# Other home addresses in SBUF for the operands of a split-fp32 transformer step

## The reference

```python
x += 1/2 * g1 * SwiGLU_1(adaLN_1(RMSNorm(x)))       # macaron half-step FFN
h  = adaLN_2(RMSNorm(x));  z = h @ w_in             # one combined projection, 8,720 columns
# branch M: bidirectional chunkwise mLSTM (4 heads, qk 128, v 256)
# branch A: windowed GQA (16 q heads, 4 kv heads, dim 64), QK norm, rotary on latent tokens
mix = (sigmoid(gate_M) * (h_M @ w_proj_m) + sigmoid(gate_A) * (h_A @ w_proj_a)) @ w_out
x += g2 * mix
x += 1/2 * g3 * SwiGLU_2(adaLN_3(RMSNorm(x)))
# shift, scale, gate of adaLN: SiLU(cond) @ ada_w + ada_b, ada_w is 2048 x 18432
```

## Time and profile before

| | |
|---|---|
| median of the runs | 2425.4 us |
| profiled execution, span from first to last instruction | 2427.3 us, 1.9 us over the median |
| TensorE busy | 2315.6 us, 95% |
| its weight loads | 1798.5 us, 74% |
| VectorE, ScalarE busy | 1249.6 us (51%), 931.9 us (38%) |
| GpSimd busy | 59.9 us, 2% |
| moved by DMA | 547.86 MB, mean 226 GB/s |

### The profile page before, as it was taken

The page is one execution under the profiler, slowest core; times in us unless marked ns, Lnnn a source line. Parts: engine busy times, 40 slices in busy tenths (PEclk is TensorE's granted clock), DMA queues, the critical chain, the costliest instruction groups (busy, mean ns, idle before and its releaser), DMA issues.

```text
span 2427.3 us, 29221 instructions
## 1 busy us (share of the span) xinstructions
PE 2315.6 (95%) x11108; PEld 1798.5 (74%) x11108; DVE 1249.6 (51%) x1289; ACT 931.9 (38%) x1083; POOL 59.9 (2%) x57
## 2 busy tenths in 40 slices
PE   5699999999999998999977999998999999999998
PEld 0277777777777776777766888787888888888886
DVE  1154455554555547444457455455455555555557
ACT  0253333333333334433445344345434444444442
POOL 0000000000000000000040000000000000000000
PEclk7699999999999998999989999999999999999999
DMA  9969788787787875789611555655555555555553
GB/s 367 330 215 323 253 285 284 253 310 264 280 289 251 304 272 191 277 297 321 231 50 42 185 193 181 202 196 175 186 196 190 190 194 190 189 190 189 191 190 112
DMA packets 273183, 547.86 MB, mean 226 GB/s; under 512 B 9022, under 2 KB 9190, under 8 KB 272880
## 3 DMA queue, kind: packets, MB, share of 16 engines
q1 hardware_dynamic: 193936, 386.36, 46.8%
q10 hardware_dynamic: 76176, 151.15, 17.2%
q0 software_dynamic: 3024, 9.71, 1.4%
HBM read 543.73 MB, written 3.46 MB: 225 GB/s over the span
## 4 chain that ended last, share of the span: by engine, by line
PE 91%; DMA 4%; DVE 3%; ACT 1%; issue 0%; ACTq 0%; DVEq 0%
PE ps L525 27%; PE ps L527 27%; PE ps L526 27%; PE ps L486 5%; DMA ada_w_sb<-in_ada_w 4%; PE ps L512 1%; PE ps L600 1%; DVE w_lo L1145 0%; PE ps L496 0%; ACTq L896 0%; PE ps L749 0%; DVE x L1276 0%; DVE acc L1274 0%; PE ps L834 0%; PE ps L730 0%
## 5 line engine op out<-in xcount | busy, mean ns | idle before, releaser
L1145 DVE TENSOR_TENSOR w_lo<-raw_w,w_hi 128x1024 fp32r<-128x1024 f32 x728 | 895.6, 1231 | 898.6 <-ACT w_hi L885 898.1
L885 ACT CAST w_hi<-raw_w 128x1024 fp32r<-128x1024 f32 x728 | 765.5, 1053 | 1246.1 <-PE ps L527 1210.5
L525 PE MATMUL ps<-w_hi,xT_hi 128*128 128x512 f32 x2080 | 823.1, 396 | 5.1 <-DVE xT_lo L1201 2.6
L527 PE MATMUL ps<-w_hi,xT_lo 128*128 128x512 f32 x2080 | 811.2, 390 | 0.0
L526 PE MATMUL ps<-w_lo,xT_hi 128*128 128x512 f32 x2080 | 811.0, 390 | 0.0
L525 PEld LDWEIGHTS ps<-w_hi,xT_hi 128*128 128x128 f32 x2080 | 391.3, 188 | 115.7 <-issue 29.3
L527 PEld LDWEIGHTS ps<-w_hi,xT_lo 128*128 128x128 f32 x2080 | 391.1, 188 | 83.0
L526 PEld LDWEIGHTS ps<-w_lo,xT_hi 128*128 128x128 f32 x2080 | 391.6, 188 | 77.5
L525 PE MATMUL ps<-w_hi,hT_hi 128*128 128x512 f32 x704 | 276.4, 393 | 5.6 <-DVE hT_lo L1215 5.6
L527 PE MATMUL ps<-w_hi,hT_lo 128*128 128x512 f32 x704 | 275.4, 391 | 0.0
L526 PE MATMUL ps<-w_lo,hT_hi 128*128 128x512 f32 x704 | 275.1, 391 | 0.0
(11 more groups left out here) (225 smaller groups left out, 867.1 us busy)
## 6 DMA issues: line engine op xcount, KB each, us to landing
raw_w<-in_ffn_wi SPq DMA_DIRECT2D x176, 1024.0 KB, 5.1
ada_w_sb<-in_ada_w ACTq DMA_DIRECT2D x144, 1024.0 KB, 9.5
raw_w<-in_ffn_wo SPq DMA_DIRECT2D x88, 1024.0 KB, 5.0
raw_w<-in_w_in SPq DMA_DIRECT2D x68, 1024.0 KB, 5.3
raw_w<-in_w_out SPq DMA_DIRECT2D x16, 1024.0 KB, 5.1
raw_w<-in_w_proj_m SPq DMA_DIRECT2D x8, 1024.0 KB, 5.0
raw_w<-in_w_proj_a SPq DMA_DIRECT2D x8, 1024.0 KB, 5.1
gate_bc<-gate_dram POOLq DMA_DIRECT2D x6, 1024.0 KB, 9.6
```

The costliest lines, as they stand in the source:

```text
L525: pe.matmul(out, a_hi, w_hi[:, slot, kk, :], start=(first and kk == 0), stop=False)
L527: mm = pe.matmul(out, a_lo, w_hi[:, slot, kk, :], start=False, stop=(last and kk == 1))
L885: act.copy(w_hi[:, us % SPL, :, :], raw_w[:, slot, 2 * half:2 * half + 2, :]).then_inc(hi_ready, 1)
L1145: dve.tensor_tensor(w_lo[:, us % SPL, :, :], raw_w[:, slot, 2 * half:2 * half + 2, :], w_hi[:, us % SPL, :, :].bitcast(F32), ALU.subtract) ...
```

## The change

BASE, SLOT and SCR are rounded up to 512 bytes instead of 64, 32 and 32. xT_lo is set 64 bytes further than its neighbour's end. Each of the four slots of w_hi and w_lo becomes a tensor of its own, with 0, 64, 128 or 288 bytes added to its place, and w_lo as a whole starts another 288 bytes on. hT_hi and hT_lo each get 128 bytes ahead of them. The scan tiles move into the room of wg, which is free only when line 648 is done; so they are filled after the wait for gT_ps. The semaphore `zeroed`, for which GpSimd waits, is now set by the fill before it. All else is the same instruction for instruction.

```diff
-        BASE = (nc.sbuf_base + 63) // 64 * 64
+        BASE = (nc.sbuf_base + 511) // 512 * 512
...
-        xT_lo = place("xT_lo", [P, KD, TOK], F32R)
+        xT_lo = place("xT_lo", [P, KD, TOK], F32R, at=top[0] + 64)
         raw_w = place("raw_w", [P, RAW, 4, CH])
-        w_hi = place("w_hi", [P, SPL, 2, CH], F32R)
-        w_lo = place("w_lo", [P, SPL, 2, CH], F32R)
+        HOMES = (0, 64, 128, 288)
+        W_AT = top[0]
+        w_hi = [place(f"w_hi{i}", [P, 2, CH], F32R, at=W_AT + 4096 * i + HOMES[i]) for i in range(SPL)]
+        L_AT = W_AT + 4096 * SPL + 288
+        w_lo = [place(f"w_lo{i}", [P, 2, CH], F32R, at=L_AT + 4096 * i + HOMES[i]) for i in range(SPL)]
...
-        SLOT = top[0]
+        SLOT = (top[0] + 511) // 512 * 512
+        top[0] = SLOT
...
-        hT_hi = place("hT_hi", [P, 4, TOK], F32R)
-        hT_lo = place("hT_lo", [P, 4, TOK], F32R)
+        hT_hi = place("hT_hi", [P, 4, TOK], F32R, at=top[0] + 128)
+        hT_lo = place("hT_lo", [P, 4, TOK], F32R, at=top[0] + 128)
...
-        SCR = top[0]
+        SCR = (top[0] + 511) // 512 * 512
+        top[0] = SCR
...
         gT = place("gT", [2 * NG, TOK], at=AFTER_ROWS)
+        scan = [place("scan0", [40, 2 * P], at=AFTER_ROWS + 1024), place("scan1", [40, 2 * P])]
...
-        scan = [place(f"scan{i}", [40, 2 * P]) for i in range(2)]
...
-                        pe.matmul(out, a_hi, w_hi[:, slot, kk, :], start=(first and kk == 0), stop=False)
-                        pe.matmul(out, a_hi, w_lo[:, slot, kk, :], start=False, stop=False)
-                        mm = pe.matmul(out, a_lo, w_hi[:, slot, kk, :], start=False, stop=(last and kk == 1))
+                        pe.matmul(out, a_hi, w_hi[slot][:, kk, :], start=(first and kk == 0), stop=False)
+                        pe.matmul(out, a_hi, w_lo[slot][:, kk, :], start=False, stop=False)
+                        mm = pe.matmul(out, a_lo, w_hi[slot][:, kk, :], start=False, stop=(last and kk == 1))
...
-            dve.memset(apad[:], 0.0)
-            for t in scan:
-                ins = dve.memset(t[:], NEG)
-            ins.then_inc(zeroed, 1)
+            dve.memset(apad[:], 0.0).then_inc(zeroed, 1)
...
             dve.wait_ge(gT_ps, 1)
+            for t in scan:
+                dve.memset(t[:], NEG)
             dve.tensor_copy(gT[:], ps[0:2 * NG, 4, 0:TOK]).then_inc(gT_ready, 1)
```

More of the change, by code:

```diff
@@ L884, in split @@
                 half = us % 2
-                act.copy(w_hi[:, us % SPL, :, :], raw_w[:, slot, 2 * half:2 * half + 2, :]).then_inc(hi_ready, 1)
+                act.copy(w_hi[us % SPL][:], raw_w[:, slot, 2 * half:2 * half + 2, :]).then_inc(hi_ready, 1)
             def ada_load(c, par, tiles=range(4)):
@@ L1144, in split @@
                 dve.wait_ge(hi_ready, us + ux + 1)
-                dve.tensor_tensor(w_lo[:, us % SPL, :, :], raw_w[:, slot, 2 * half:2 * half + 2, :],
-                                  w_hi[:, us % SPL, :, :].bitcast(F32), ALU.subtract).then_inc(lo_ready, 1)
+                dve.tensor_tensor(w_lo[us % SPL][:], raw_w[:, slot, 2 * half:2 * half + 2, :],
+                                  w_hi[us % SPL][:].bitcast(F32), ALU.subtract).then_inc(lo_ready, 1)
             def ada_rows(c, par, uses):
```

## The result

The changed kernel took 2458.97 us (median of 2 runs, 2458.27 to 2459.66), the kernel before 2425.4: a ratio of 1.0136, 95% interval 1.0106 to 1.0165. It is slower by 33.6 us. The forecast was 2365, and the sign was wrong; the time is close to the one that the third rival gave (2461).

A forecast was written before the change was run, and what follows sets the result against it. TensorE's weight matmuls were taken as the bound, DMA only in the first 120 us. Span: 2427.3 - 55.7 - 5.1 + 0.55 = 2367.0 us; less 1.9 for the profiled execution, 2365. Range of 8 in 10: 2328 to 2461.

The forecast's parts named there:

- the third rival: Weight matmuls never settle as homes change and stay at 231 ns: 36 us more, 2461 us in all; chance 0.25.
- What bounds the kernel, and where a change would show: TensorE's weight matmuls, lines 525 to 527, 81% of the span; change shows in start-to-start pace, not idle time.
- That addresses reach the pace: Weight matmuls: 226.7 ns with xT and hT, 233.3 with hcT, whose home lies 32 bytes further from the stationary operand.
- (a): New homes of weights and xT, with hT's counted in: pace 226.7 to 220.0 ns on 8,352 matmuls, 55.7 us won.
- Rule against row: Two skill rules weighed against trace rows: one would give 0.55 us of loss, the other a span of 2329 us.
- (b): hcT moved to a 512-byte boundary: 384 matmuls go from 233.3 to 220.0 ns, 5.1 us won.
- (d): Fill of scan moved between the wait for gT_ps and the copy of gT: 0.55 us added.
- (e): raw_w and adaLN tile, DMA targets, at new homes: zero; first 120 us at worst 7 us either way.
- (f): VectorE and ScalarE read and write w_lo and w_hi at other homes: zero, unless their times grow by half.

## Why the prediction was wrong

*What bounds the kernel, and where a change would show*: right. Everything but the head's gain and 2.7 us in the pauses lies in the time from start to start of the three lines; the idle times ahead of these lines and the splits' means stayed.

*That addresses reach the pace*: right, and the two rows that said so are both points of the table, distance 0 and distance 224 modulo 256.

*The step that failed is (a)*: "with equal homes every matmul meets the next load in the same way, and today's lock sits on a bad spot; with eight different homes some pairs will clear and some won't", and from it 220.0 ns. Today's lock, at distance 0, is the best spot of all eight, and no pair clears: the mean pace of the xT stage went to 231.6 ns and not to 220.0. I halved the 13.4 ns over 213.3 as if they were to be had; the only lower pace in the trace was the norm's, of another type and shape, while both measurements of the right instruction, 233.3 at another home and 231 off the rhythm, were higher than today's. The table comes near the size. In a four-unit round the moving w_hi meet xT_hi at 64, 128, 192 and 96 (from 352), w_lo meet xT_lo at 32, 96, 160 and 64: two times the mean of the first four, 232.2, and once that of the others, 232.4, make 232.3; measured 231.6. In the same way hT comes to 231.5 (measured 232.1) and hcT to 232.6 (232.1). The reckoning misses by almost 4 ns where w_lo alone is off, so it is no rule for any mix of homes. One reading in (a) was wrong too: not all 8,736 got another distance. w_hi's slot 1 and hT_hi both lie at 128, so 352 matmuls with hT kept distance 0. And the far end of the forecast's own range, 226 ns, comes to 2417.6 us, not 2419.

*The third rival* had the time, and its mechanism in part. That it is off by only 2 us is partly luck: it gave 36 us to the steps within the stages, which grew by 38.2, and nothing to the head and the pauses, which shrank. It held that a change of home keeps the matmuls from settling, at 231. Where the home changes only from unit to unit they do settle, in about five matmuls, but at their distance's own pace, which is worse at every distance but 0. Where it changes from w_hi to w_lo the pace is above what the distances give, 232.6 against 228.9 in the mean of the whole run with w_lo off, and 231.1 against 226.7 in hT with w_lo at 64. The other support of that rival, 32 bytes off a multiple of 64, was wrong in itself.

*Rule against row.* By the Trainium skill, SBUF — State Buffer, section "SBUF: two separate sides", TensorE never waits for another user of SBUF, and the pace would not have changed; the changed kernel and the one with all homes equal, which differ in offsets alone, stand at 2458.97 and 2419.64 us, 1.6% apart. By the Trainium skill, TensorE: Matmul & The Clock Gate, section "Wait — 56ns, not 53.3ns?", with its 2.5 ns over the columns, the pace would be 215.7 ns; no home on a multiple of 32 got there, the best was 226.6.

*(b)* was right in kind and void in place: hcT left its old distance (224 modulo 256) but went to others, 232.1. With all homes equal it won its 2.5 us. *(d)* 0.55 forecast, 0.49 measured. *(e)* priced at nothing and kept at up to 7 us in the range, was a gain of 6.3 us in the profile, 3 to 4 of it by the adaLN tile's home. The queue's share per MB over the span was the wrong row: it averages over 2300 us in which nobody waits for these loads, while in the head 16 engines at 0.95 are the bound. And it compared homes at 128 and 160, which are both off a multiple of 256. *(f)* right.

The range reached to 2461 and held the time; 0.55 of the chance lay on the faster side of no change, the 0.25 of the right rival was less than half of that.

## What to carry to other kernels

Where fp32r matmuls of this shape run back to back, give the moving tiles and the stationary tiles homes that agree modulo 256 bytes, all of them, and check it by the starts of matmuls in a steady stretch and not by their durations: 32 to 224 bytes of disagreement cost 2 to 8 ns of 227 here. Shifts that differ within the three matmuls cost more than the distances alone would say. Try tiles that a DMA-bound stretch loads on a multiple of 256; in this one it gave 366 to 371 GB/s in place of 347 to 355. And when a lock is measured at one point, ask for the nearest measurements of the same instruction before taking the middle between it and a bound.

## What was not expected of the hardware

Homes set up to 3.3% of TensorE's pace (226.7 to 234.2 ns) with no wait that any view shows, and they do so with a period of 256 bytes: 226.7 ns at 0 and 256. At one distance two steady paces occur, 229 and 233 ns, with the same code and homes. Why 226.7 and 233.3 are 34 and 35 times 6.67 ns is not known; 228.9, 232.5 and 234.2 are no such multiples. What makes up the 13.4 ns over the column time at the best distance, and whether homes that are no multiple of 32 or another order of the three matmuls could win some of it, stays open: it wasn't tried. The fastest versions found, 0.9971 and 0.9976 of the kernel before, owe it to the head and to hcT, about 3 and 2.5 us of the 6.
